# Where transposes write and when they are issued: a decoder layer with 32 experts on one core

## The chip, the cores and the metric

One core of a Trainium2 chip runs the whole program. The metric is device time in microseconds (us), the median of several executions. Before the change: 1196.56 us, the median of three runs (1193.06, 1196.56 and 1196.57).

## The reference

264 tokens (256 prompt tokens and 8 sample tokens) of width 1024 pass through one layer in float32. Cut to what matters:

```python
x = x + mixer(rmsnorm(x))                        # gating with 128x128 weights, short convolution
x = x + cross_attn(rmsnorm(x), mk, mv)           # 4 heads of 256, 256 memory tokens
# mixture of experts:
top_logit, top_e = lax.top_k(xt @ w_router + b_router, 4)     # of 32 experts
gates = softmax(top_logit)
gu = xb @ w1[e] + b1[e]                          # 1024 -> 2048, the tokens of expert e
gate, up = minimum(gu[:, :1024], 7), clip(gu[:, 1024:], -7, 7)
y = ((up + 1) * gate * sigmoid(1.702 * gate)) @ w2[e] + b2[e] # 1024 -> 1024
x = x + sum over the 4 experts of a token of gates * y
y = rmsnorm(x) * g_final
```

The weights of an expert are 12.58 MB, so the 32 experts are 403 MB of the 458 MB that are moved.

## The kernel before

**The front.** Activations lie feature-major (128 features on the partitions, tokens along a row). Projections go through `project` (line 1084) into eight PSUM banks that are used in turn; the list `GROUPS` gives the order, `grp` counts filled banks and `emptied` counts banks copied out. `begin(name)` makes TensorE wait until the bank's former group is out. In cross-attention the order on TensorE is: scores of the prompt (line 1167), scores of the sample tokens (1177), transposes of the probabilities `pT0` to `pT3` (1186), the products `o0` to `o3` with the values (1192), a transpose of the sample's probabilities (1201), `o4`, `o5`, the sample's values (1211). VectorE takes the sample's maximum (lines 863, 864), waits for ScalarE's exponential (608), inverts its sum and scales (866, 867), and only then copies the four transposed probability banks (870).

**Router and gather.** Logits are formed on the raw residual (1231, 1236). The token rows are transposed into `htok0` to `htok5` (1246, four transposes each) and copied by ScalarE to `h_tok` with the token's norm as the scale (626). These copies also permute the columns: within 256 columns the even features come first, then the odd ones, since weight rows are laid out two to a partition. Ranks within experts come from a matmul with a triangular matrix (1263, 1266), one-hot matrices from VectorE (930), and `gather` (1281) multiplies `h_tok` by them: it gives, feature-major, the up to 64 tokens of each of two experts. It waits for all six copies (`tok_copied`).

**Weights.** SyncE issues all weight loads in order into eight buffers ("units") of 2 MB, six units for an expert: four for gate and up, two for down. A unit's load waits until its buffer's former content is used (`w_used`, `gu_done`, `d_done`). The first eight units come during the front. For the next eight each half of a buffer is reloaded once it is used (`half_used`, line 428).

**The expert loop.** `four_experts` runs for eight groups of four; the last group is its `final` form. In step e TensorE does the gate/up matmuls of expert e+1 (four units `u`, line 1307) and then the down matmuls of expert e (line 1425). Between the units stands side work: `turn_gate_up(e)` transposes the gate/up result of expert e (1318), `combine_two` scatters results of the pair before (1298), `gather_half` gathers half of the features for the next pair of experts (1281). For odd i the second half of the gathered features is made right after unit 0, and unit 2 is the first to read it:

```python
if i % 2 and u % 2 == 0:
    pe.wait_ge(side_copied, twin * 3 + 3 + u // 2)      # line 1386
```

The transposed gate/up result goes to VectorE's `swiglu` (bias 975, limit 980, product 988). ScalarE's order within a step is fixed as well. For odd i it is

```python
sigmoid(e)                                              # line 658: waits for swiglu's limited gate (g_ready)
act.wait_ge(side_filled, pos + 2)                       # line 661
copy_gathered(nxt, 1)                                   # line 662: gives side_copied
```

**The last experts.** For expert 30 (`early`) the transposes of expert 31 come after all its gate/up matmuls and ahead of the down matmuls of expert 30. The down matmuls of expert 31 (1414) follow, then the last combine (1439), the final norm and the stores.

Of the kernel before, what the change touches and what calls it, by code (L numbers as in the profile page):

```python
# [12 lines left out]
P = 128  # L13
# [7 lines left out]
HEADS = 4  # L21
# [8 lines left out]
ROWS_GU = 2  # L30
# [53 lines left out]
def build(nc, x_t, mem_t, w_k, w_v, w_in, w_out, w_q, w_xo, kc, vc, w_gu, w_dn, params, ws_t,  # L84
# [3 lines left out]
    with ExitStack() as ctx:  # L88
# [3 lines left out]
        def sem(name):  # L92
            return ctx.enter_context(nc.semaphore(name))
# [118 lines left out]
        def bank(name):  # L212
            return ps[:, G[name] % 8, :]
# [54 lines left out]
        pd_ready = sem("pd_ready")  # L268
        max_ready = sem("max_ready")
        s_exp = sem("s_exp")  # L270
        os_ready = sem("os_ready")
        lt_zero = sem("lt_zero")
        ex_in = sem("ex_in")
# [264 lines left out]
        def _(act):  # L538
# [82 lines left out]
            for n in range(6):  # L621
                rows = P if n < 4 else NS
                act.wait_ge(grp, G[("htok", n)] + 1)
                by_row = h_tok[n // 2][0:rows, 512 * (n % 2):512 * (n % 2) + 512].rearrange(
                    "t (b j p) -> t b p j", b=2, j=ROWS_GU)
                nc.scalar.activation(by_row, bank(("htok", n))[0:rows].rearrange("t (b p j) -> t b p j", b=2, j=ROWS_GU),  # L626
                                     ACT.Copy, scale=rstd_tok[0:rows, n // 2:n // 2 + 1]).then_inc(tok_copied, 1)
            act.wait_ge(ex_in, 1)
            nc.scalar.activation(ex[:], ex[:], ACT.Exp).then_inc(ex_out, 1)
# [70 lines left out]
        def _(dve):  # L700
# [161 lines left out]
                normalise(n)  # L862
            link(nc.vector.tensor_reduce(att_m[:, 8:9], filled("sS", NMEM), AX.X, ALU.max))
            TS(att_m[:, 8:9], att_m[:, 8:9], -1.0 / 16.0, None, ALU.mult).then_inc(max_ready, 1)
            dve.wait_ge(s_exp, 5)
            link(nc.vector.reciprocal(att_s[:, 8:9], att_s[:, 8:9]))
            TS(s_s[:], s_s[:], att_s[:, 8:9], None, ALU.mult).then_inc(emptied, 1)
            dve.wait_ge(kv_stored, 32)
            for h in range(HEADS):
                copy(probs_t[:, h, :, :], filled(("pT", h)).rearrange("p (m q) -> p m q", m=2)).then_inc(emptied, 1)  # L870
            def attended(m):
                copy(o_fm[:, m, 0:NP_], filled(("o", m), NP_)).then_inc(emptied, 1)

# [165 lines left out]
        def _(pe):  # L1039
# [10 lines left out]
            def begin(name):  # L1050

                if G[name] >= 8:
                    before_it = GROUPS[G[name] - 8]
                    if before_it[0] == "htok":
                        pe.wait_ge(tok_copied, before_it[1] + 1)
                    else:
                        pe.wait_ge(emptied, G[name] - 7)
                return bank(name)
# [128 lines left out]
                last.then_inc(grp, 1)  # L1187
            def attend(m):
                b = begin(("o", m))
                pe.wait_ge(emptied, G[("pT", m // 2)] + 1)  # L1190
                for mt in range(2):
                    last = mm(b[:, 0:NP_], v_mem[:, mt, P * m:P * m + P], probs_t[:, m // 2, mt, :],  # L1192
                              start=(mt == 0), stop=(mt == 1))
                last.then_inc(grp, 1)
# [46 lines left out]
            def to_tokens(n):  # L1241
                b = begin(("htok", n))
                width = P if n < 4 else NS
                pe.wait_ge(h_ready, 2 * KT + (8 if n % 2 else 4))
                for f in range(4):
                    last = turn(b[0:width, P * f:P * f + P],
                                h_fm[:, 4 * (n % 2) + f, P * (n // 2):P * (n // 2) + width], ident[:])
                last.then_inc(grp, 1)

# [94 lines left out]
            def four_experts(it, final):  # L1344

                for i in range(4):
                    e, twin = it * 4 + i, it * 2 + i // 2

                    def unit(n):
                        number = STEP_AT[i] + n  # L1350
                        if RING_UNITS <= number < 2 * RING_UNITS:
                            pe.wait_ge(half_landed[number % RING_UNITS], 16)
                        pe.wait_ge(unit_landed[number % RING_UNITS], it * 48 + 16 * (number // RING_UNITS + 1))
                        return unit_buffer(number % RING_UNITS)

                    pos = twin * 3 + 2 * (i % 2)
                    if i % 2 == 0:
                        pe.wait_ge(side_copied, pos + 1)
                        pe.wait_ge(w_built, twin + 1)
                        for t in range(TT):  # L1360
                            width = P if t < 2 else NS
                            last = turn(ps[:, 5, P * t:P * t + width], w_hot[0:width, t, :],
                                        ident[0:width, 0:width])
                        last.then_inc(side_filled, 1)
                        pos = pos + 1
                    early = final and i == 2

                    def gather_half():
                        pe.wait_ge(side_copied, pos + 1)
                        pe.wait_ge(p_built, twin + 2)  # L1370
                        gather(ps[:, 5, :], i % 2).then_inc(side_filled, 1)

                    def combine_two(e, i, r):
                        if i % 2 == 0 and r == 0:
                            pe.wait_ge(y_left, e + 1)
                            pe.wait_ge(y_right, e + 1)
                        for n in (r, r + 1):
                            combine(e * 4, n, 4 * (i % 2) + n, 1 - i // 2)

                    if early:  # L1380
                        combine_two(e, i, 0)
                    if not (final and i == 3):
                        pe.wait_ge(gu_copied, e + 1)
                        for u in range(4):
                            if i % 2 and u % 2 == 0:
                                pe.wait_ge(side_copied, twin * 3 + 3 + u // 2)
                            first, last = gate_up_unit(unit(u), u, xg[((i + 1) // 2) % 2], (i + 1) % 2)
                            if i == 0:
                                first.then_inc(half_used, 1)
                            last.then_inc(w_used if u < 3 else gu_done, 1)  # L1390
                            if u == 0:
                                turn_gate_up(e)
                                if i % 2:
                                    gather_half()
                                if early:
                                    combine_two(e, i, 2)
                            elif u < 3:
                                if early:
                                    combine_two(e + 1, i + 1, 2 * u - 2)
                                else:  # L1400
                                    combine_two(e, i, 2 * u - 2)
                    if early:
                        turn_gate_up(e + 1)

                    pe.wait_ge(hid_ready, e + 1)
                    if final and i == 3:
                        pe.wait_ge(side_copied, turns * 6 + 5)
                        for part, (k, k_end) in enumerate(LAST_PARTS):
                            w = unit_buffer((STEP_AT[3] + k // 4) % RING_UNITS)
                            pe.wait_ge(last_landed[part], 16)  # L1410
                            for k in range(k, k_end):
                                for h in range(2):
                                    at = D * (k % 4) + 512 * h
                                    last = mm(ps[64 * h:64 * h + 64, LAST_BANK, :], hid[1][:, k, :], w[:, at:at + 512],  # L1414
                                              start=(k == 0), stop=(k == KT - 1))
                        last.then_inc(d_done, 1)
                        continue
                    pe.wait_ge(y_left, e + 1)
                    pe.wait_ge(y_right, e + 1)
                    for u in range(2):  # L1420
                        w = unit(4 + u)
                        for k in range(4 * u, 4 * u + 4):
                            for h in range(2):
                                at = D * (k % 4) + 512 * h
                                last = mm(ps[64 * h:64 * h + 64, 4, :], hid[i % 2][:, k, :], w[:, at:at + 512],  # L1425
                                          start=(k == 0), stop=(k == KT - 1))
                        last.then_inc(d_done if u else w_used, 1)
                        if u == 0 and i % 2 == 0 and not (final and i == 2):
                            gather_half()
# [87 lines left out]
```

## Time and profile before

| | |
|---|---|
| median of three runs | 1196.56 us |
| the profiled execution, its own time | 1195.74 us |
| its span in the trace | 1193.9 us |
| mean granted TensorE clock | 0.997 |
| TensorE busy | 1157.0 us (97%) |
| VectorE, ScalarE, GpSimd busy | 306.9, 157.7, 28.2 us |
| read from HBM | 454.41 MB |

The profiled execution's own time is 1.84 us more than its span, which begins with its first and ends with its last recorded instruction. Times in all rows are microseconds from the start of the span. PE is TensorE's matmuls, PEld its weight loads, DVE is VectorE, ACT ScalarE, POOL GpSimd and SPq the queue from which SyncE issues DMAs. A float32 matmul of the program is two records on PE, a transpose is one. L1307 is line 1307 of the kernel.

### The profile page before, as it was taken

To read this page: it belongs to the slowest core of one execution; us is meant where nothing else is said; L and a number is where in the kernel's file an instruction comes from. 1 tells how busy PE (TensorE), PEld (TensorE's weight loads), DVE (VectorE), ACT (ScalarE), POOL (GpSimd) and SP (SyncE) were. 2 spreads that over 40 slices of the span, in tenths; PEclk is the share of its full clock that TensorE was granted. 3 is DMA by queue.
4 is the path that set the end of the run, shared out by engine and by line. 5 is a ranking of instruction groups with operands and counts; after the bars stand their busy time and mean duration, and the time that the engine had idled before them with its cause. 6 is when DMAs were issued, how large, how long until landed. Compare 5 with 4: busy or idle time off the path is not lost.

```text
span 1193.9 us, 14908 instructions
## 1 busy us (share of the span) xinstructions
PE 1157.0 (97%) x5937; PEld 604.6 (51%) x5937; DVE 306.9 (26%) x638; ACT 157.7 (13%) x242; POOL 28.2 (2%) x63
## 2 busy tenths in 40 slices
PE   9999999999999999999999999999999999999997
PEld 8888888784434344444444343434343434343433
DVE  5124533332121212122222212121212121212124
ACT  2011011031101210121021011101110111010102
POOL 0000000000000000000000000000000000000000
PEclk9999999999999999999999999999999999999999
DMA  9963444998999999999999999999999999999995
GB/s 366 398 238 129 131 155 150 427 390 335 426 426 428 428 428 429 428 428 430 428 429 427 429 429 429 428 428 429 428 429 428 428 430 428 430 427 428 428 428 221
DMA packets 40398, 458.34 MB, mean 384 GB/s; under 512 B 6032, under 2 KB 6800, under 8 KB 8496
## 3 DMA queue, kind: packets, MB, share of 16 engines
q1 hardware_dynamic: 37440, 454.12, 90.7%
q10 hardware_dynamic: 2928, 3.80, 1.0%
q8 instruction: 21, 0.34, 0.1%
q14 instruction: 9, 0.07, 0.0%
HBM read 454.41 MB, written 3.23 MB: 383 GB/s over the span
## 4 chain that ended last, share of the span: by engine, by line
PE 72%; DMA 25%; DVE 1%; ACT 1%; issue 0%; SPq 0%; DVEq 0%; ACTq 0%
PE ps L1307 25%; PE ps L1084 15%; DMA ring<-in_w_dn 14%; PE ps L1425 13%; DMA arena<-in_w_dn 8%; PE ps L1281 7%; PE ps L1298 3%; DMA ring<-in_w_gu 3%; PE ps L1111 2%; PE ps L1318 2%; PE ps L1192 1%; DMA ring<-in_w_k 1%; PE ps L1177 1%; PE ps L1211 1%; PE ps L1167 1%; PE ps L1414 1%
## 5 line engine op out<-in xcount | busy, mean ns | idle before, releaser
L1307 PE MATMUL ps<-ring,arena 128*64 128x512 f32 x1536 | 349.9, 597 | 5.6 <-DMA ring<-in_w_gu 4.8
L1307 PEld LDWEIGHTS ps<-ring,arena 128*64 128x64 f32 x1536 | 103.1, 136 | 200.6 <-issue 184.7
L1084 PE MATMUL ps<-arena,ring 128*128 128x264 f32 (+1 forms) x800 | 178.9, 385 | 0.0
L1425 PE MATMUL ps<-ring,arena 128*64 128x512 f32 x736 | 165.4, 595 | 9.4 <-DMA ring<-in_w_dn 9.4
L1084 PEld LDWEIGHTS ps<-arena,ring 128*128 128x128 f32 x800 | 151.8, 190 | 25.3 <-issue 0.2
L1307 PE MATMUL ps<-arena 128*64 128x512 f32 x512 | 116.9, 598 | 2.8 <-DMA arena<-in_w_gu 2.4
L1020 DVE COPY arena<-ps 64x512 f32<-64x512 f32 x31 | 21.5, 694 | 369.1 <-PE ps L1425 369.1
L1425 PEld LDWEIGHTS ps<-ring,arena 128*64 128x64 f32 x736 | 52.7, 137 | 112.9 <-issue 106.8
L962 DVE TENSOR_TENSOR resid<-resid,ps 128x264 f32<-128x264 f32 x128 | 53.1, 429 | 173.3 <-PE ps L1298 172.8
L1281 PEld LDWEIGHTS ps<-arena 128*128 128x128 f32 x768 | 90.1, 195 | 14.8 <-issue 14.8
L1281 PE MATMUL ps<-arena 128*128 128x128 f32 x768 | 94.5, 280 | 1.8 <-ACT arena L626 1.8
L975 DVE TENSOR_TENSOR arena<-ps,par 128x512 f32<-128x512 f32 x64 | 44.0, 688 | 141.9 <-PE ps L1318 141.9
L638 ACT ACTIVATE arena<-ps 128x1024 f32<-128x1024 f32 x31 | 31.8, 1024 | 366.1 <-PE ps L1307 366.1
L1298 PE MATMUL ps<-arena 128*128 128x264 f32 x256 | 74.0, 412 | 0.6 <-DVE arena L1020 0.4
L1298 PEld LDWEIGHTS ps<-arena 128*128 128x128 f32 x256 | 43.4, 189 | 55.2 <-issue 50.0
L1307 PEld LDWEIGHTS ps<-arena 128*64 128x64 f32 x512 | 33.9, 136 | 64.9 <-issue 60.3
L1425 PE MATMUL ps<-arena 128*64 128x512 f32 x256 | 58.3, 597 | 5.0 <-DMA arena<-in_w_dn 5.0
L1318 PEld LDWEIGHTS ps<-ident,arena 128*128 128x128 f32 x256 | 33.4, 210 | 27.2 <-issue 27.2
L646 ACT ACTIVATE arena<-arena 128x512 f32<-128x512 f32 x32 | 20.2, 630 | 161.3 <-DVE arena L980 161.3
L1318 PE MATMUL ps<-ident,arena 128*128 128x128 f32 x256 | 39.5, 297 | 1.2 <-ACT arena L638 1.2
L682 ACT ACTIVATE arena<-ps 64x512 f32<-64x512 f32 x31 | 18.3, 590 | 143.4 <-PE ps L1425 143.4
L1425 PEld LDWEIGHTS ps<-arena 128*64 128x64 f32 x256 | 17.3, 137 | 39.1 <-issue 29.7
(201 smaller groups left out, 504.4 us busy)
## 6 DMA issues: line engine op xcount, KB each, us to landing
ring<-in_w_gu SPq DMA_DIRECT2D x92, 2048.0 KB, 32.6
ring<-in_w_dn SPq DMA_DIRECT2D x44, 2048.0 KB, 32.9
arena<-in_w_gu SPq DMA_DIRECT2D x32, 2048.0 KB, 33.7
arena<-in_w_dn SPq DMA_DIRECT2D x14, 2048.0 KB, 32.8
ring<-in_w_in SPq DMA_DIRECT2D x10, 1024.0 KB, 27.5
ring<-in_kc SPq DMA_DIRECT2D x8, 1024.0 KB, 4.8
ring<-in_vc SPq DMA_DIRECT2D x8, 1024.0 KB, 5.1
ring<-in_w_gu SPq DMA_DIRECT2D x8, 1024.0 KB, 8.8
```

The source lines that it names most:

```text
L638: nc.scalar.activation(gu_sb.rearrange("p (a b) -> p a b", a=2), ps[:, 0:2, :], ACT.Copy).then_inc(gu_copied, 1)
L646: nc.scalar.activation(sig[:], tb[:, :, 0:SLOTS], ACT.Sigmoid, scale=ALPHA).then_inc(sig_ready, 1)
L962: TTN(resid[:, m, :], resid[:, m, :], ps[:, 6 + m % 2, 0:T], ALU.add).then_inc(c_added, 1)
L975: TTN(both[:, :, h, :].rearrange("p (b m) s -> p b m s", b=2), turned[:, :, h, :].rearrange("p (b m) s -> p b m s", b=2), bc(bias, 3, [P, ...
L1020: copy(y_hot[row:row + 64, i // 2, 512:1024], ps[64:128, 4, :]).then_inc(y_right, 1)
L1084: last = mm(b[:, 0:width], w[:, k, P * (m % 2):P * (m % 2) + P], source(k), start=(k == 0), stop=(k == KT - 1))
L1111: last = mm(b[:, 0:256], mem[:, k, P * t:P * t + P], w[:, k, :], start=(k == 0), stop=(k == KT - 1))
L1281: last = mm(b[:, P * at:P * at + P], h_tok[t][:, first:first + P], p_hot[:, t, :], start=(t == 0), stop=(t == TT - 1))
L1298: mm(ps[:, 6 + m % 2, 0:T], y_hot[:, pair, P * m:P * m + P], g_hot[:, pair, :], start=True, stop=True).then_inc(c_filled, 1)
L1307: last = mm(ps[64 * h:64 * h + 64, bank + n, :], tile[:, k, SLOTS * half:SLOTS * half + SLOTS], w[:, at:at + 512], start=(k == 0), stop=(k ...
L1318: last = turn(ps[:, 2 + f // 4, P * (f % 4):P * (f % 4) + P], gu_sb[:, first:first + ROWS_DN * (P - 1) + 1:ROWS_DN], ident[:])
L1425: last = mm(ps[64 * h:64 * h + 64, 4, :], hid[i % 2][:, k, :], w[:, at:at + 512], start=(k == 0), stop=(k == KT - 1))
```

## The change

Five edits:

1. The transposes for `htok` write the permuted order themselves: within each 256 columns of the PSUM bank, transpose f writes its even features to one run of 64 and its odd ones to another run of 64, 128 columns further. ScalarE's copies then are straight.
2. VectorE copies `pT0` and `pT1` ahead of the sample's reciprocal and scaling, `pT2` and `pT3` behind them. The copies count on a new semaphore, `probs_copied`; `emptied` rises by five at the scaling.
3. For odd i, `turn_gate_up(e)` moves from behind unit 0 to behind unit 1 (`gather_half` stays behind unit 0).
4. For odd i, the two `combine_two` move from behind units 1 and 2 to behind units 2 and 3.
5. For expert 30, `turn_gate_up(31)` moves from ahead of the wait for `hid_ready` into the down matmuls of expert 30, behind the first two k steps.

No line of ScalarE's `four_experts` or of SyncE's program changes.

```diff
-                by_row = h_tok[n // 2][0:rows, 512 * (n % 2):512 * (n % 2) + 512].rearrange(
-                    "t (b j p) -> t b p j", b=2, j=ROWS_GU)
-                nc.scalar.activation(by_row, bank(("htok", n))[0:rows].rearrange("t (b p j) -> t b p j", b=2, j=ROWS_GU),
+                nc.scalar.activation(h_tok[n // 2][0:rows, 512 * (n % 2):512 * (n % 2) + 512], bank(("htok", n))[0:rows],
                                      ACT.Copy, scale=rstd_tok[0:rows, n // 2:n // 2 + 1]).then_inc(tok_copied, 1)
...
+            dve.wait_ge(kv_stored, 32)
+
+            def copy_probs(h):
+                copy(probs_t[:, h, :, :], filled(("pT", h)).rearrange("p (m q) -> p m q", m=2)).then_inc(probs_copied, 1)
+
+            for h in range(2):
+                copy_probs(h)
             dve.wait_ge(s_exp, 5)
             link(nc.vector.reciprocal(att_s[:, 8:9], att_s[:, 8:9]))
-            TS(s_s[:], s_s[:], att_s[:, 8:9], None, ALU.mult).then_inc(emptied, 1)
-            dve.wait_ge(kv_stored, 32)
-            for h in range(HEADS):
-                copy(probs_t[:, h, :, :], filled(("pT", h)).rearrange("p (m q) -> p m q", m=2)).then_inc(emptied, 1)
+            TS(s_s[:], s_s[:], att_s[:, 8:9], None, ALU.mult).then_inc(emptied, 1 + HEADS)
+            for h in range(2, HEADS):
+                copy_probs(h)
...
+                    elif before_it[0] == "pT":
+                        pe.wait_ge(probs_copied, before_it[1] + 1)
...
-                pe.wait_ge(emptied, G[("pT", m // 2)] + 1)
+                pe.wait_ge(probs_copied, m // 2 + 1)
...
                 for f in range(4):
-                    last = turn(b[0:width, P * f:P * f + P],
+                    pair = b[0:width, 2 * P * (f // 2):2 * P * (f // 2) + 2 * P]
+                    by_row = pair.rearrange("t (j h i) -> t h i j", j=ROWS_GU, h=2)[:, f % 2]
+                    last = turn(by_row,
                                 h_fm[:, 4 * (n % 2) + f, P * (n // 2):P * (n // 2) + width], ident[:])
...
-                            if u == 0:
+                            if i % 2:
+                                if u == 0:
+                                    gather_half()
+                                elif u == 1:
+                                    turn_gate_up(e)
+                                else:
+                                    combine_two(e, i, 2 * u - 4)
+                            elif u == 0:
                                 turn_gate_up(e)
-                                if i % 2:
-                                    gather_half()
                                 if early:
                                     combine_two(e, i, 2)
...
-                    if early:
-                        turn_gate_up(e + 1)
...
                         for k in range(4 * u, 4 * u + 4):
+                            if early and k == 2:
+                                turn_gate_up(e + 1)
                             for h in range(2):
```

## Rows read from the trace of the kernel before

**Rows 1.** The page: busy tenths of DMA, and GB/s, in 40 slices.
```profile
DMA  9963444998999999999999999999999999999995
GB/s 366 398 238 129 131 155 150 427 390 335 426 426 428 428 428 429 428 428 430 428 429 427 429 429 429 428 428 429 428 429 428 428 430 428 430 427 428 428 428 221
```

**Rows 2.** Windows: engines' busy us (instructions), granted clock, DMA share, GB/s.
```profile
265.00:270.00 5.00, 4.29 (x24) 4.32 (x24) 1.55 (x9) 2.18 (x3) 0.00 (x0) 0.66 0.26 95
270.00:275.00 5.00, 5.00 (x27) 1.71 (x25) 0.59 (x2) 0.00 (x0) 1.03 (x2) 1.00 0.36 93
```

**Rows 3.** Timeline from 203 us: start, us, engine, operation, count, [idle before <- releaser].
```profile
211.54 0.15 DVE L864 TENSOR_SCALAR arena<-arena 128x1 f32<-128x1 f32 x1
212.80 2.48 DVE L870 COPY arena<-ps 128x512 f32<-128x512 f32 x4
213.63 3.69 PE L1192 MATMUL ps<-arena 128*128 128x256 f32 x16 [0.71 <-DVE arena L870]
```

**Rows 4.** Timeline from 254 us, same columns.
```profile
259.88 2.38 PE L1246 MATMUL ps<-ident,arena 128*128 128x128 f32 x20
263.12 0.83 PE L1271 MATMUL ps<-arena,ones 128*128 128x32 f32 x6
263.60 0.70 DVE L930 TENSOR_TENSOR arena<-slot_no,rank 128x128 f32<-128x128 f32 x3
265.71 4.54 PE L1281 MATMUL ps<-arena 128*128 128x128 f32 x24 [1.76 <-ACT arena L626]
272.16 7.40 SPq L428 DMA_DIRECT2D arena<-in_w_dn x4
```

**Rows 5.** By line, ns min/median/max, start of first and last: `htok` copies, gathered copies.
```profile
L626 ACT ACTIVATE arena<-ps,rstd_tok x6: 1085/1137/1180, 259.9 to 264.5; 128x512 f32<-128x512 f32 x4, 8x512 f32<-8x512 f32 x2
L641 ACT ACTIVATE arena<-ps x30: 597/597/598, 312.3 to 1123.1; 128x512 f32<-128x512 f32 x30
```

**Rows 6.** Timeline from 308 us (TensorE, ScalarE, VectorE): the odd step of expert 1.
```profile
319.21 1.23 PE L1318 MATMUL ps<-ident,arena 128*128 128x128 f32 x8
320.28 2.84 PE L1281 MATMUL ps<-arena 128*128 128x128 f32 x24
327.72 3.65 PE L1307 MATMUL ps<-ring,arena 128*64 128x512 f32 x16
...
321.80 0.63 ACT L646 ACTIVATE arena<-arena 128x512 f32<-128x512 f32 x1 [5.32 <-DVE arena L980]
...
320.62 0.69 DVE L975 TENSOR_TENSOR arena<-ps,par 128x512 f32<-128x512 f32 x1 [4.03 <-PE ps L1318]
321.34 0.43 DVE L980 TENSOR_SCALAR arena<-arena 128x512 f32<-128x512 f32 x1
```

**Rows 7.** The chain that ended last, in order of time: start us, us, what.
```profile
275.99 1.34 PE ps L1281 x12
312.26 3.58 PE ps L1425 x16
336.05 6.87 PE ps L1425 x32
367.42 3.58 PE ps L1425 x16
1139.99 3.67 PE ps L1425 x16
```

**Rows 8.** Timeline from 1150 us: transposes of expert 31.
```profile
1165.78 1.23 PE L1318 MATMUL ps<-ident,arena 128*128 128x128 f32 x8 [1.20 <-ACT arena L638]
1179.44 0.14 PEld L1414 LDWEIGHTS ps<-ring,arena 128*64 128x64 f32 x2 [0.29 <-DMA ring<-in_w_dn]
```

**Rows 9.** Waits over the span: who waited for whom, us in total, times, longest.
```profile
PE ps L1425 <- DMA ring<-in_w_dn: 9.4, 12, 1.3
```

**Rows 10.** us from issue to landing, min/median/max: line 366, 309 to 345; line 366, all.
```profile
DMA to landing us min/median/max: 10.2/12.6/13.8
...
DMA to landing us min/median/max: 10.2/32.6/35.4
```

More of the change, by code:

```diff
@@ L270, in build @@
         s_exp = sem("s_exp")
+        probs_copied = sem("probs_copied")
         os_ready = sem("os_ready")
```

## The prediction

> **What bounds the kernel now.** I began with the page's slices [rows 1]. The reader is to see three stages: loads at 129 to 155 GB/s in slices 4 to 7, full from the eighth on, and one dent in the ninth and tenth (390 and 335 GB/s). From there to the end the rate stands at 426 to 430 GB/s. An expert pair is 25.17 MB, so at 428 GB/s the loads take 58.8 us for a pair.
>
> The dent is the hand-over from the front to the experts: the first eight units have landed and no buffer is free until TensorE has used half a unit. The windows [rows 2] show 95 and 93 GB/s from 265 to 275 us, and the first reload is issued at 272.16 [rows 4]. Before it TensorE waits 1.76 us for ScalarE's `htok` copies, then gathers at a clock that is granted at 0.66 on average from 265 to 270 us: part of the time at 1.2 GHz in place of 2.4.
>
> The chain of waits [rows 7] shows the loop. The second down unit of expert 0 starts at 312.26, that of expert 2 at 367.42: 55.16 us for a pair. That is TensorE's own time, with no wait in it, and 3.6 us less than the loads need. The second down unit of expert 29 starts at 1139.99. TensorE alone would need from 312.26: 14 pairs x 55.16 = 772.2, and half a pair from expert 0 to expert 1, 336.05 + 6.87/2 - 312.26 = 27.2; together 799.5. It took 827.7. So 28.2 us of waiting for loads lie in it, all late: TensorE starts some 22 us behind the landed data and catches up only after six pairs. **Its waits for loads are a cover of 28.2 us for the whole loop, not of 3.6 us in each pair.** That difference decides this case.
>
> **Probabilities ahead of the softmax.** VectorE now waits for the exponential between line 864 (ends 211.69) and the copies (212.80) [rows 3]. With the transposes of `pT0` done by about 211.6, the first copy starts at 211.75 and ends some 0.65 later; TensorE starts `o0` at 212.6 and not at 213.63. What follows comes with it: the third product needs the second copy, the fourth the scaling at 213.8, both in time. VectorE's own sum is unchanged, its four products' copies keep up within 0.1. Gain 1.0 us. The wait for the stored keys and values stands further ahead now, long satisfied; the second pair of copies is queued behind the exponential, and `o4`, which needs it, comes 4 us later.
>
> **Straight copies.** A permuting copy takes 1137 ns, a straight one of the same shape 597 [rows 5]. Copies follow the transposes then and end near 263.4 in place of 265.6. The gather's next limit is the one-hot matrices (263.60 to 264.30) and the counting matmuls (to 263.95) [rows 4]: it starts near 264.1, 1.6 us earlier. With the idle time gone I take the clock as kept; 12 gather matmuls at full clock take 1.34 us [rows 7], so 24 take 2.7 in place of 4.54: 1.8 us more. TensorE also reads two loop counts between the gather and the first gate/up matmuls, which the slow gather covers and a fast one may not; no row prices it, from 0 to 1 us, and I take 0.4. Gain 3.0 (2.0 to 3.4).
>
> What the transposes lose by writing with steps of 128 elements no row of TensorE shows. The bound below is nothing (20 transposes run in 2.38 us [rows 4], 0.12 each, and a new order of writes makes them no faster). The bound above is the ratio that steps cost ScalarE, 1137/597 = 1.9, on 24 transposes: 24 x 0.12 x 0.9 = 2.6 us. I take nothing, a judgement: ScalarE's steps lie in SBUF, TensorE's in PSUM, and no row couples the two. 2.6 stays in the range.
> The Trainium skill (SBUF — State Buffer, section Door 1: The DMA port swizzle) speaks against this edit: it says that any non-contiguous access to PSUM slows matmuls significantly. It gives no figure. By that rule the transposes would take at least twice as long, and the front's gain would fall from 4.0 to about 1.4.
>
> Front together: 1.0 + 3.0 = 4.0 us earlier, for TensorE and for the reload chain. The load queue itself ran dry by 268, so reloads at about 268.2 still find it empty.
>
> **Transposes of odd experts.** This is the step that costs. Follow one odd step now [rows 6]. Transposes start at 319.21; the gather behind them starts at 320.28, 1.07 later. VectorE adds the bias from 320.62, limits the gate until 321.77, ScalarE's sigmoid runs from 321.80 to 322.43. Next in ScalarE's fixed order is the copy of the gathered half, which unit 2 needs; with unit 1 (3.6 us) in between, nobody waits: unit 2 starts at 327.72.
> After the change unit 1 comes first and the transposes right ahead of unit 2. The gathered half has been in PSUM for over 4 us, but its copy stands behind the sigmoid, the sigmoid behind VectorE's limit, and that behind the transposes. From their start: 1.41 to the bias, 2.56 to the end of the limit, 3.22 to the end of the sigmoid, then a copy of 0.60 that starts as the sigmoid drains (3.79) and 0.12 for the signal: unit 2 starts 3.91 after the transposes' start in place of 1.07. **Stall 2.84 us**, in each of the 15 odd experts with a next one (1, 3, ..., 29): 42.6 us. Queued behind it on TensorE are unit 2, the combines and the down matmuls; nothing fills it.
> The pair then takes 55.16 + 2.84 = 58.0 us, still below the 58.8 of the loads, so TensorE stays behind the landed data all the way: it makes up 0.8 us a pair, 11 us in 14 pairs, of the 22 it starts behind. It never gets to wait for a load. So of 42.6 us 28.2 are covered, 14.4 come out.
> The loads don't suffer in turn: the shallowest queue near the first odd expert is 10.2 us from issue to landing [rows 10], a stall of 2.84 leaves several us of it.
> The combines move by one unit; VectorE's four additions still end during unit 3 or the 7 us of down matmuls. Nothing.
>
> **The clock in these stalls.** In the one place where TensorE stood idle for 1.76 us the clock fell, for 3.4 us at half rate, thus 1.7 us lost [rows 2, 4]. The longest wait for a down unit was 1.3 us, amid dense matmuls [rows 9], and it never fell there. A stall of 2.84 us amid dense matmuls is longer than both. Price: 0 to 15 falls x 1.7 = 25.5 us. I take two, 3.4 us: a fall shifts everything behind it, and the next stalls need not meet the same conditions. That is a judgement, and the widest part of my range.
>
> **Transposes of expert 31.** TensorE waits 1.20 us for ScalarE's copy ahead of them [rows 8]; two k steps of expert 30's down matmuls (a quarter of 6.87 us [rows 7]) now stand in this gap. The transposes then end 2.9 us into a stretch of 8.0, and VectorE's six operations of 0.4 to 0.7 us [rows 6] fit into the 5.1 that are left, so the last down matmuls don't wait. By TensorE 1.2 us are gained. In the kernel before the last load lands about when it is needed (the wait ahead of 1179.44 [rows 8]), which would leave only 0.2; but TensorE now is over 10 us behind the loads, so I count 1.2.
>
> **Sum**, against the profiled execution's own 1195.74 us: - 4.0 (front) + 42.6 - 28.2 (stalls less cover) + 3.4 (clock) - 1.2 (end) = + 12.6: 1208.3 us. The median is 0.8 above the profiled execution, the lowest run 2.7 below it. I say 1208.5.
>
> **Rivals.**
> A. The forecast: stalls outlast the cover. Own range 1203 to 1216. Chance 0.62.
> B. The clock falls after most stalls: 10 to 15 falls in place of two, each 1.7: 1222 to 1230. For it: the fall after the 1.76 us gap. Against: no fall after the gaps of 1.3 us. Chance 0.15.
> C. Not slower: the stalls vanish in TensorE's waits for loads. Place: unit 2 of odd experts. If the loads, not TensorE, set the end of the loop, a stall of 2.84 fits into the 3.6 us of a pair, and the kernel ends with its load stream, 4.0 + 0.2 earlier: 1191.5. It decides from the point where the stock of 22 us that TensorE starts behind is used up; a stall below 28.2/15 = 1.9 us, as with a sigmoid that runs sooner, would bring this about. For it: full loads in every slice [rows 1]. Against: the addition above. Chance 0.09.
> D. Strided writes slow the transposes, on top of A: twice the time adds 2.6 (1211), four times 8.6 (1217). For it speaks ScalarE's 1.9 [rows 5]. Chance 0.14. This is also what the rule of the Trainium skill (SBUF — State Buffer, section Door 1: The DMA port swizzle) would give.
>
> **How the numbers follow.** A to D sum to one. 1199 to 1224 holds A and D whole, a third of B and little of C: about 0.8. What a measurement tells from no change is 0.3%, 3.6 us. Faster is C less a part that ends within it: 0.08; same 0.03; slower 0.89.
>
> **What would show it.** In the profile after: TensorE idle 2.8 us ahead of unit 2's matmuls in each odd expert, released by ScalarE's copy at line 641, with the sigmoid right ahead of that copy; a pair of 58 us from the start to the end, and hardly any waits for loads; clock falls counted in the granted clock; `htok` copies of about 0.6 to 0.7 us, a gather near 263 without a gap; `o0` 1.0 earlier; transposes at 0.12 us. I would be wrong if the copy of the gathered half ran ahead of the sigmoid, if pairs came out at 58.8 with waits for loads, or if the clock fell in most stalls.

## The result and the profile after

The changed kernel takes 1226.93 us (median of four runs, 1224.2 to 1228.33) against 1196.3 before: ratio 1.0255, 95% interval 1.0243 to 1.0268. It is slower by 30.6 us, the direction that was forecast, but outside the range of 1199 to 1224. The profiled execution took 1228.18 us, its span is 1226.3: 32.4 more than the span before.

The page's slices after, with the same columns as [rows 1]:

```profile
DMA  9953345999999999999999999999999999999970
GB/s 369 392 215 138 139 140 216 428 367 415 393 415 418 425 416 430 416 430 429 428 424 431 405 431 413 429 420 431 413 430 409 428 418 429 415 429 415 428 297 36
```

The loads no longer run at 428 in every slice. From slice 10 on they dip to between 393 and 420 in about every second slice, and the last two slices move 297 and 36 GB/s: the weights are in long before TensorE is done.

The front, windows as in [rows 2], the timelines as in [rows 3, 4], and the copies as in [rows 5]:

```profile
265.00:270.00 5.00, 4.97 (x27) 2.30 (x27) 1.26 (x6) 0.00 (x0) 1.03 (x2) 1.00 0.51 133
270.00:275.00 5.00, 5.00 (x31) 2.57 (x29) 0.84 (x2) 0.00 (x0) 0.00 (x0) 1.00 0.98 357
```
```profile
211.25 0.15 DVE L863 TENSOR_SCALAR arena<-arena 128x1 f32<-128x1 f32 x1
211.43 1.29 DVE L867 COPY arena<-ps 128x512 f32<-128x512 f32 x2
212.46 3.62 PE L1200 MATMUL ps<-arena 128*128 128x256 f32 x16
...
258.64 2.38 PE L1256 MATMUL ps<-ident,arena 128*128 128x128 f32 x20
262.80 2.92 PE L1291 MATMUL ps<-arena 128*128 128x128 f32 x24
267.71 7.41 SPq L429 DMA_DIRECT2D arena<-in_w_dn  x4
```
```profile
L625 ACT ACTIVATE arena<-ps,rstd_tok x6: 662/681/688, 258.7 to 261.6; 128x512 f32<-128x512 f32 x4, 8x512 f32<-8x512 f32 x2
```

The front is as forecast: products start at 212.46 in place of 213.63, the copies take 681 ns in place of 1137, the gather has no gap ahead of it and takes 2.92 in place of 4.54, and the first reload is issued 4.45 us earlier. The 20 transposes take 2.38 us in both kernels.

Three odd stalls with different outcomes (experts 1, 3 and 9), TensorE, and ScalarE in the first:

```profile
321.22 1.23 PE L1328 MATMUL ps<-ident,arena 128*128 128x128 f32 x8
324.99 5.35 PE L1317 MATMUL ps<-ring,arena 128*64 128x512 f32 x16 [2.53 <-ACT arena L640]
...
381.03 1.23 PE L1328 MATMUL ps<-ident,arena 128*128 128x128 f32 x8
384.86 5.00 PE L1317 MATMUL ps<-arena 128*64 128x512 f32 x16 [2.60 <-ACT arena L640]
...
559.95 1.23 PE L1328 MATMUL ps<-ident,arena 128*128 128x128 f32 x8
563.71 3.65 PE L1317 MATMUL ps<-ring,arena 128*64 128x512 f32 x16 [2.53 <-ACT arena L640]
```
```profile
323.82 0.63 ACT L645 ACTIVATE arena<-arena 128x512 f32<-128x512 f32 x1 [11.78 <-DVE arena L986]
324.35 0.58 ACT L640 ACTIVATE arena<-ps 128x512 f32<-128x512 f32 x1
```
```profile
322.00:330.00 8.00, 5.47 (x20) 1.71 (x19) 3.53 (x6) 1.11 (x2) 0.00 (x0) 0.79 0.95 406
```
```profile
PE ps L1317 <- ACT arena L640: 38.5, 15, 2.6
```

Here is the stall, against [rows 6]: the sigmoid (L645) runs at 323.82, the copy of the gathered half (L640) right behind it, and only then unit 2. It happens 15 times, 38.5 us in all. The other thing to see is the duration of unit 2's 16 matmuls: 5.35 and 5.00 us behind the first two stalls, 3.65 behind the third. In the window from 322 to 330 us the clock is granted at 0.79 on average, so 1.7 of 8 us are lost. After 14 of the 15 stalls unit 2 is slow, after one it is not. Where it takes 5.00 to 5.13 us and not 5.35, the clock falls while TensorE still idles (at expert 3 it is granted at 0.70 from 384.0 to 384.5 us), so a part of the slow stretch costs nothing.

The chain of waits gives the pairs, as in [rows 7]:

```profile
307.82 3.58 PE ps L1440 x16
367.62 3.58 PE ps L1440 x16
427.14 3.58 PE ps L1440 x16
...
546.54 3.58 PE ps L1440 x16
604.64 3.58 PE ps L1440 x16
```

59.80 and 59.52 us for pairs with a clock fall, 58.10 for the one without, and no wait for a load in the loop. At the end, the transposes of expert 31 stand inside the down matmuls of expert 30, without the gap of [rows 8]:

```profile
1198.10 1.89 PE L1440 MATMUL ps<-ring,arena 128*64 128x512 f32 x8
1199.92 1.23 PE L1328 MATMUL ps<-ident,arena 128*128 128x128 f32 x8
```

### The profile page after: what moved, and what is told of

Read it like the earlier page. It is cut to its first block, busy times and chain, and to the rows that moved or that the text cites. A ratio compares the mean times of both kernels' runs of the same rounds, so it can differ in the third digit from the quotient of the medians.

```text
span 1226.3 us, 14909 instructions
## 1 busy us (share of the span) xinstructions
PE 1177.0 (96%) x5937; PEld 607.9 (50%) x5937; DVE 306.6 (25%) x638; ACT 153.8 (13%) x242; POOL 28.1 (2%) x63
## 4 chain that ended last, share of the span: by engine, by line
PE 95%; DVE 2%; ACT 1%; issue 1%; DMA 1%; SPq 0%; DVEq 0%; ACTq 0%
PE ps L1317 39%; PE ps L1440 18%; PE ps L1092 14%; PE ps L1291 8%; PE ps L1308 6%; PE ps L1328 3%; PE ps L1119 2%; DVE arena L981 1%; ACT arena L640 1%; PE ps L1372 1%; PE ps L1200 1%; PE ps L1219 1%; PE ps L1185 1%; PE ps L1175 1%; PE ps L1427 1%
## 5 line engine op out<-in xcount | busy, mean ns | idle before, releaser
L1317 PE MATMUL ps<-ring,arena 128*64 128x512 f32 x1536 | 360.6, 613 | 20.2 <-ACT arena L640 20.2
L1440 PE MATMUL ps<-ring,arena 128*64 128x512 f32 x736 | 164.4, 595 | 0.0
L1317 PE MATMUL ps<-arena 128*64 128x512 f32 x512 | 128.2, 647 | 18.3 <-ACT arena L640 18.2
L1317 PEld LDWEIGHTS ps<-arena 128*64 128x64 f32 x512 | 37.1, 146 | 85.2 <-issue 84.1
L1440 PE MATMUL ps<-arena 128*64 128x512 f32 x256 | 58.1, 595 | 0.0
L645 ACT ACTIVATE arena<-arena 128x512 f32<-128x512 f32 x32 | 20.2, 630 | 252.8 <-DVE arena L986 252.8
L516 POOL TENSOR_TENSOR arena<-arena,gate 128x384 f32<-128x384 f32 x17 | 14.1, 832 | 901.2 <-DVE arena L741 876.6
```

The source lines that it names most:

```text
L645: nc.scalar.activation(sig[:], tb[:, :, 0:SLOTS], ACT.Sigmoid, scale=ALPHA).then_inc(sig_ready, 1)
L1317: last = mm(ps[64 * h:64 * h + 64, bank + n, :], tile[:, k, SLOTS * half:SLOTS * half + SLOTS], w[:, at:at + 512], start=(k == 0), stop=(k ...
```

## The experiments

All kernels were timed beside the kernel before; its median was 1195.0 us in the first group of runs, 1195.74 in the second, 1195.27 in the third.

**Copy ahead of the sigmoid.** The changed kernel with ScalarE's order swapped in odd steps:

```diff
-                    if not (final and i == 3):
-                        sigmoid(e)
-                    if not (final and i >= 2):
-                        if i % 2:
-                            act.wait_ge(side_filled, pos + 2)
-                            copy_gathered(nxt, 1)
+                    if i % 2 and not (final and i >= 2):
+                        act.wait_ge(side_filled, pos + 2)
+                        copy_gathered(nxt, 1)
+                    if not (final and i == 3):
+                        sigmoid(e)
+                    if not (final and i >= 2):
```

> The changed kernel, but in odd steps ScalarE copies the gathered half ahead of the sigmoid. Theory (unit 2 waits for a copy that stands behind the sigmoid, and the clock falls in that wait): no idle time ahead of unit 2, no clock fall in the loop, pairs set by the loads (58.7 us), the front's 4.2 us and 0.2 of the end kept: about 1191.5 us, 35 below the changed kernel. Rival (the new order of side work itself costs TensorE its time or its clock): stays above 1215 us.

Measured: 1191.32 us, ratio to before 0.9967 (0.9956 to 0.9979), 35.6 below the changed kernel. Its timeline, ScalarE and TensorE around expert 1, and its chain:

```profile
318.49 0.60 ACT L640 ACTIVATE arena<-ps 128x512 f32<-128x512 f32 x1 [5.71 <-PE ps L1291]
324.56 0.63 ACT L645 ACTIVATE arena<-arena 128x512 f32<-128x512 f32 x1 [5.47 <-DVE arena L986]
```
```profile
321.97 1.23 PE L1328 MATMUL ps<-ident,arena 128*128 128x128 f32 x8
323.13 3.65 PE L1317 MATMUL ps<-ring,arena 128*64 128x512 f32 x16
```
```profile
308.56 3.58 PE ps L1440 x16
312.14 3.43 PE ps L1317 x16
...
332.54 7.02 PE ps L1440 x32
...
364.06 3.58 PE ps L1440 x16
...
419.57 3.58 PE ps L1440 x16
```

The copy now runs 6 us ahead of the sigmoid, and unit 2 follows the transposes at once. The theory holds to 0.2 us. A pair of TensorE's own work takes 55.50 us here, 0.34 more than the 55.16 before: that is what the new order of side work costs by itself. The chain shows where they lie. A run of 16 unit matmuls takes 3.43 us where matmuls of the same shape stand ahead of it and 3.58 where another kind does; in odd steps a combine now stands ahead of the down matmuls, which take 7.02 in place of 6.87 [rows 7]. The other 0.19 are the transposes and the gather: side by side they took 3.85 us, apart they take 4.04.

**The odd moves alone.** The kernel before with edits 3 and 4 of the change:

> The kernel before with only the moves in odd experts (edits 3 and 4). Theory: 15 stalls of 2.84 us less the 28.2 us of load waits that cover them, and 14 clock falls of 1.6 us (22.4): 36.8 more than before, about 1233 us. Rival (the front's edits have a part in the loss): clearly less than 1233, under 1225 us.

Measured: 1232.66 us (1221.39 to 1234.88), ratio 1.0326 (1.0308 to 1.0343). The median is where the theory had it, and 5.7 above the changed kernel, which has the gains of the front and the end (5.6 in the table below). The spread of 13.5 us was new; the profiled execution is the fastest, 1221.39. Windows of its trace, and two stalls:

```profile
300.00:850.00 550.00, 526.92 (x2621) 225.59 (x2617) 112.56 (x210) 66.11 (x92) 9.25 (x18) 1.00 1.01 427
850.00:1190.00 340.00, 323.96 (x1539) 134.46 (x1538) 74.80 (x141) 38.67 (x55) 6.17 (x12) 0.97 0.98 413
```
```profile
387.53 3.65 PE L1307 MATMUL ps<-arena 128*64 128x512 f32 x16 [2.61 <-ACT arena L641]
...
852.70 5.35 PE L1307 MATMUL ps<-arena 128*64 128x512 f32 x16 [2.61 <-ACT arena L641]
```

The same gap of 2.61 us cost nothing at 387 and 1.7 us at 852. In this execution the clock stayed full in the loop until 850 and then fell after each stall, six times.

**The same kernel and the changed one again.**

> The kernel before with edits 3 and 4 once more, for a second profile. Theory (the number of clock falls differs from execution to execution, and with it the time): time = 1209 us + 1.6 us for each fall in the loop plus what both share; with 13 falls 1233 us, with 6 again 1221 us. Rival (the spread has another source): a time that doesn't go with the falls.

> The changed kernel once more, for a second profile. Theory: 13 to 15 falls at 1224 to 1229 us. Rival: another number of falls at the same time.

Measured: the odd moves alone 1218.38 us, with five falls in the loop, the first after expert 1's stall and four after 960:

```profile
300.00:960.00 660.00, 631.79 (x3127) 269.08 (x3126) 137.25 (x256) 80.68 (x112) 11.34 (x22) 1.00 1.00 426
960.00:1190.00 230.00, 217.90 (x1039) 91.43 (x1039) 50.32 (x96) 25.24 (x36) 4.12 (x8) 0.97 0.96 407
```

The other profile had six and one more in the front. Two falls fewer, 3.0 us less: time goes with falls. With 14 or 15 in the loop the sum is 1221.4 + 8 or 9 x 1.56 (the mean of 1.70 and 1.42) = 1234 to 1235, the upper end of its runs. Those runs have no profile of their own, but the mean clock of each is on record and goes the same way: 0.991 at 1218.38 us, 0.989 at 1221.39, 0.982 at 1229.13, and 0.978 or 0.979 in the three from 1232.66 to 1234.88. The changed kernel took 1228.63, again with 14 falls after the same 14 stalls.

**The changed kernel without its odd moves.** Edits 1, 2 and 5 alone:

> The changed kernel with edits 3 and 4 undone: the new front and the moved transposes of expert 31 alone. Theory: loop as before, set by the loads; front 4.2 us earlier, end 0.2: about 1191.8 us, the same as with the copy ahead of the sigmoid. Rival (the gain at the end is the whole 1.2 us of idle time that goes): 1190.8 us and a last wait for a load gone; rival (strided writes): no gain in the front, 1196 us.

Measured: 1191.31 us, ratio 0.9971 (0.996 to 0.9983), the same as with the copy ahead of the sigmoid. The rival with slow strided writes, 1196 us, lies outside the interval. The other, 1190.8 us, the time can't tell, but it wanted the last wait for a load gone, and the trace still has it:

```profile
1172.67 3.65 PE L1422 MATMUL ps<-ring,arena 128*64 128x512 f32 x16 [0.37 <-DMA ring<-in_w_dn]
```

**Dummy matmuls in the stall.** Three kernels, with N of 11, 5 and 2; the dummies add nothing to the result:

```diff
+                            if i % 2 and u == 2:
+                                pe.wait_ge(c_added, e * 4 + 1)
+                                keep_busy(ps[:, 6, :], N)
                             if i % 2 and u % 2 == 0:
                                 pe.wait_ge(side_copied, twin * 3 + 3 + u // 2)
```

> The changed kernel, with 11 dummy matmuls of 128 columns (about 2.4 us, into a bank that is free then) ahead of unit 2's wait in odd steps; they add nothing to the result. Theory (the clock falls because TensorE idles in the stall): unit 2 starts as late as before, idle gaps shrink to under 0.5 us, no clock fall, 22 us less than the changed kernel: about 1204.5 us. Rival (the clock falls for another reason, or thin matmuls don't hold it): falls stay, 1227 us; or the dummies delay unit 2: more.

> As the run with 11 dummy matmuls, with 5 (1.1 us): unit 2 starts as late, the idle gap is about 1.45 us. Theory (what counts is the idle share, and gaps of 1.3 us were harmless in the kernel before): no clock falls, about 1207 us. Rival (any gap above 1.34 us costs a fall): 14 falls, 1228 us.

> As the run with 11 dummy matmuls, with 2 (0.44 us): the idle gap is about 2.1 us. Theory: falls after some of the 15 stalls, fewer than the 14 of the changed kernel: between 1210 and 1225 us. Rival (a sharp limit above 2.1 us): none, 1207 us.

Measured: 1207.09, 1206.81 and 1208.41 us (ratios 1.0100, 1.0094 and 1.0106, intervals within 0.0017). Timelines around expert 1's stall, one fence for each kernel from 11 to 2, and expert 3's in the last:

```profile
322.85 2.62 PE L1054 MATMUL ps<-ones 128*128 128x128 f32 x22
325.54 3.65 PE L1317 MATMUL ps<-ring,arena 128*64 128x512 f32 x16
```
```profile
322.78 1.28 PE L1054 MATMUL ps<-ones 128*128 128x128 f32 x10
325.48 3.65 PE L1317 MATMUL ps<-ring,arena 128*64 128x512 f32 x16 [1.41 <-ACT arena L640]
```
```profile
322.57 0.61 PE L1054 MATMUL ps<-ones 128*128 128x128 f32 x4
325.26 5.35 PE L1317 MATMUL ps<-ring,arena 128*64 128x512 f32 x16 [2.08 <-ACT arena L640]
...
385.14 3.65 PE L1317 MATMUL ps<-arena 128*64 128x512 f32 x16 [2.16 <-ACT arena L640]
```

Unit 2 starts as late as in the changed kernel, 3.77 us after the transposes; only what TensorE does meanwhile differs. With 11 and with 5 dummies no stall cost clock. With 2, and gaps of 2.08 to 2.16 us, two of 15 did. The expectation for 2 (1210 to 1225) was too high. The 20 us between the first two kernels and the changed one are the clock: the profiled executions with 11 dummies and without lie 21.3 us apart, the 14 falls come to 21.8, and the stalls themselves stay.

**Two combines in the stall.**

```diff
                                 elif u == 1:
                                     turn_gate_up(e)
-                                else:
-                                    combine_two(e, i, 2 * u - 4)
+                                    combine_two(e, i, 0)
+                                elif u == 2:
+                                    combine_two(e, i, 2)
```

> The changed kernel, but in odd steps the first two combines stay right behind the transposes, ahead of unit 2 (the other two behind unit 2). They fill 1.1 us of the stall with work that is due anyway. Theory (loads cover 28.2 us over the loop, and a gap under 1.5 us costs no clock): 15 x (2.84 - 1.11) = 26 us are covered, TensorE catches up with the loads just before the end, no clock falls: 1191.5 us, as with the copy ahead of the sigmoid. Rival (gaps of 1.4 us still cost clock): 14 falls x 1.6 more, of which only 2 us are covered: about 1210 us.

Measured: 1193.14 us, ratio 0.998 (0.9971 to 0.999).

```profile
323.30 1.05 PE L1308 MATMUL ps<-arena 128*128 128x264 f32 x4
326.00 3.65 PE L1317 MATMUL ps<-ring,arena 128*64 128x512 f32 x16 [1.64 <-ACT arena L640]
```

Gaps of 1.64 to 1.71 us remain in each odd step, and none cost clock. The kernel still is not slower than before. A pair takes 56.91 us until the waits for loads set in, 1.75 above the 55.16 before, and 15 x 1.75 = 26 us vanished in the cover of 28.2, as its expectation had it. Its time is 1.6 us above the 1191.5 that was expected; no run shows why. This is the working point of rival C, reached by making the stall shorter.

**Edit 5 undone** in the version with the copy ahead of the sigmoid:

> The version with the copy ahead of the sigmoid, with edit 5 undone (transposes of expert 31 ahead of the down matmuls of expert 30 again). Theory (the last load sets the end there): 0.2 us slower than with edit 5, not to be told by the time, and no wait for the last load's landing as long as with it. Rival (the idle 1.2 us ahead of the transposes is on the path): 1.2 us slower, 1192.5.

Measured: 1192.13 us, ratio 0.9969 (0.9959 to 0.9979), against 0.9967 with edit 5: no difference to be told, though intervals of 1.2 us to either side don't exclude the rival's 1.2 either. TensorE with edit 5, then without:

```profile
1169.24 3.60 PE L1427 MATMUL ps<-ring,arena 128*64 128x512 f32 x16
1173.21 3.65 PE L1427 MATMUL ps<-ring,arena 128*64 128x512 f32 x16 [0.36 <-DMA ring<-in_w_dn]
```
```profile
1161.60 1.23 PE L1328 MATMUL ps<-ident,arena 128*128 128x128 f32 x8 [1.20 <-ACT arena L637]
```

Where loads set the end, a part of the 1.20 us turns into waits for the last loads. From the start of expert 31's last unit to the last combine TensorE takes 20.44 us without edit 5 and 19.91 with it (1157.42 to 1177.33), 0.5 less; in the changed kernel, which has no such wait, it takes 19.18.

**Front edits one at a time**, on the kernel before:

> The kernel before with edit 1 alone (transposes write the permuted order, straight copies). Theory: gather starts 1.7 us earlier after lg and runs at full clock, together 3.2 us, all of which the loads' restart passes on to the end: 3.2 us faster. Rival (the clock had not fallen in most executions of the kernel before): 1.5 us faster.

> The kernel before with edit 2 alone (probabilities copied ahead of the sample's scaling). Theory: the front is 1.0 us earlier and the end too: 1.0 us faster, hardly to be told from nothing. Rival (loads in the front, full from 209 us on, hold it): nothing.

Measured: edit 1 1192.89 us, ratio 0.9979 (0.997 to 0.9989), which is 1.3 to 3.6 us faster, with the theory's 3.2 and the rival's 1.5 both inside. The mean clock of each run says why. Of the 19 executions of the kernel before in this group ten have 0.998 or 0.999 (median 1194.34 us) and nine 0.995 to 0.997 (median 1196.14): 1.8 us apart, what one fall costs. All ten with edit 1 have 0.998 or 0.999. Against the first kind the gain is 1.45 us, against the second 3.25: both expectations hold, each for its half of the executions. Edit 2 1194.7, ratio 1.0001 (0.999 to 1.0012): not told from nothing. But eight of its ten executions have the lower clock, and compared like with like it is faster: 1192.95 against 1194.34 us at the higher clock, 1194.77 against 1196.14 at the lower. That comparison was made afterwards and rests on few runs. Its trace shows one of the two at the higher clock. The gap ahead of the gather is there as in [rows 4], but the clock is not down (windows and timeline):

```profile
264.00:269.00 5.00, 4.38 (x32) 3.38 (x34) 1.98 (x9) 2.08 (x3) 0.89 (x2) 1.00 0.64 220
```
```profile
264.62 2.92 PE L1291 MATMUL ps<-arena 128*128 128x128 f32 x24 [1.77 <-ACT arena L627]
```

So the fall behind this gap is an event of some executions, not of all.

## Why the prediction was right in its mechanism and wrong in a size

**The sum, term by term** (profiled executions, us):

| term | predicted | measured |
|---|---|---|
| front | - 4.0 | - 4.4 |
| stalls, 15 | + 42.6 | + 39.0 (2.60 each: 58.10 less 55.50) |
| new order of side work itself | 0 | + 5.1 (0.34 each) |
| cover by waits for loads | - 28.2 | - 28.2 (all of it: no wait for a load is left in the loop) |
| clock | + 3.4 | + 21.8 (7 falls of 1.70, 7 of 1.42) |
| end | - 1.2 | - 1.2 |
| sum | + 12.6 | + 32.1 (spans: + 32.4) |

**What failed** is one step, the clock: "I take two, 3.4 us: a fall shifts everything behind it, and the next stalls need not meet the same conditions." There were 14. The argument bounds nothing. In the odd moves alone nine stalls in a row went without a fall and then six had one each; in the other execution the first had one, ten had none and four had one each; in the changed kernel nearly every stall met a fall. So falls come in runs, and what decides between a run with and a run without is not shown. What stood in the rows was a fall after the only gap above 1.3 us [rows 4, 9], and the stalls were longer than that gap. By the rows the middle of 0 to 15 would have been the least to take; even that gives about 1218. Rival B, at 0.15, was the result.

**The stall** was right in place, chain and count. Its size was 0.24 high. Unit 2 starts 3.77 us after the transposes' start and not 3.91: the copy ends at 3.71 in place of 3.79, and the signal takes 0.06 in place of 0.12, a figure for which the prediction had no row. The rest is what the transposes take with unit 2 behind them, 1.16 and not the 1.07 that they took ahead of the gather. Against that stands the order's own cost of 0.34 a pair, which I had counted as nothing. That the two errors nearly cancel (42.6 forecast, 44.1 measured) is luck.

**The cover** was right, and it was the decisive step. A stall of 2.6 us compared with the slack of 3.6 us in a pair looks harmless. Summed over the loop, TensorE starts 22 us behind the landed data, and its waits for loads come to 28.2 us. The run with combines in the stall (26 us, not slower) and those with 11 and 5 dummies (pairs of 58.15 us, 45 in all, 11 to 12 slower) lie on either side of that figure.

**Front.** The copies ended about as forecast, and the gather took 2.92 where I had 2.7. I had taken 0.4 off for the loop counts that TensorE reads, for which no row stood; the gather passes to unit 0 without a gap, so they cost nothing. The profiled execution before was one with the fall, so its 4.4 us are the larger of two values. 0.3 of the 4.4 stand ahead of the change, in when the first loads land. Strided writes of the transposes cost nothing: 2.38 us for 20 in both kernels. By the rule that I weighed from the Trainium skill (SBUF — State Buffer, section Door 1: The DMA port swizzle), they should have slowed; for float32 transposes with steps of 128 elements the measurement decides against it. That section gives no figure; the "at least twice" of the prediction was my own estimate, from ScalarE's ratio of 1.9. ScalarE's copies, whose steps lie in SBUF, do agree with what the same section of the Trainium skill says of SBUF, that an access that crosses to a new line pays: 1137 ns with steps, 681 without.

**End.** In the changed kernel the 1.2 us are gained, because TensorE is late against the loads. In the versions without the stall at most half is. Both were in the working.

The best version is the changed kernel with the copy ahead of the sigmoid, or without its odd moves: 1191.3 us, 0.3% under the kernel before. The moves themselves bring nothing that could be told.

## What to carry to other kernels

When work moves on one engine, follow its results through the fixed order of every other engine: here an operand lay ready in PSUM for over six microseconds, behind a sigmoid that waited for the moved transposes. Compare a repeated stall with the waits that it can hide in over the whole loop, not per turn, since an engine that runs behind its loads has no slack until it has caught up. And price an idle gap of TensorE with the clock from the gaps that the trace shows, at the middle of its range or above, not with a hopeful count.

## What the runs showed of the hardware

- Idle gaps and TensorE's clock (1.2 in place of 2.4 GHz for a stretch that costs 1.4 to 1.7 us), between dense float32 matmuls: gaps of 1.41 to 1.71 us, 30 of them in two kernels, no fall; 2.08 to 2.16 us, 2 falls in 15; 2.53 to 2.61 us, 14 of 15 in one kernel, 6 and 5 of 15 in two executions of another. The length of the gap makes a fall likely, and does not decide it.
- A gap of 1.8 us behind thin matmuls (32 to 96 columns) cost the clock in one execution and not in another. The kernel before varies from 1193 to 1198 us, and its runs fall into two kinds by their mean clock: in the last group 0.998 or 0.999 at a median of 1194.34 us, 0.995 to 0.997 at 1196.14.
- 1.1 us of dummy matmuls at the start of a wait of 2.5 us kept the clock after all 15 waits, and gave 20 us in a kernel of 1227.
- A run of matmuls that stands behind another kind costs about 0.15 us more than one behind its own kind (3.58 in place of 3.43 us for a unit's 16, 7.02 in place of 6.87 for 32).
